# Loads of the first phase held back, the activation table loaded at once, statistics moved between down projections, a second diagonal buffer

## The reference

```python
h = h + 0.5 * swiglu(rmsnorm(h, g_ffn1), w_ffn1_gate, w_ffn1_up, w_ffn1_down)
u = rmsnorm(h, g_mix)
c_q, ckv_pe, q_s, k_s, v_s = split(u @ w_in)            # 1024 -> 1184
o_mla = mla_group(c_q, ckv_pe, ...)    # 8 heads, causal, low-rank q and kv, rotary part
o_swa = swa_group(q_s, k_s, v_s, sinks, rel_bias)        # 8 heads, window 128, sinks, bias
h = h + concat(rmsnorm(o_mla), rmsnorm(o_swa)) @ w_o
h = h + 0.5 * swiglu(rmsnorm(h, g_ffn2), w_ffn2_gate, w_ffn2_up, w_ffn2_down)
return rmsnorm(h, g_final)
```

## Time and profile before

| | us |
|---|---|
| median of 3 runs | 5028.68 (5026.57 to 5029.12) |
| the profiled execution, its own time | 5025.74 |
| its span on the slowest core | 5024.2 (cores: 5007.0 to 5024.2) |
| TensorE matmuls busy | 4873.9 |
| VectorE / ScalarE busy | 2806.6 / 1896.1 |
| DMA packets, mean rate | 751.86 MB, 150 GB/s |

### The profile page before, as it was taken

How to read it: one execution, slowest core, us unless ns; L and a number is a source line. 1 busy time by engine, 2 the same in 40 slices (tenths; PEclk the granted TensorE clock), 3 DMA queues, 4 the chain that set the end, 5 groups by cost and what they waited for, 6 DMA issues and landing times.

```text
span 5024.2 us, 93692 instructions; the slowest of 8 cores (5007.0 to 5024.2 us)
## 1 busy us (share of the span) xinstructions
PE 4873.9 (97%) x29784; PEld 2355.2 (47%) x29784; DVE 2806.6 (56%) x6312; ACT 1896.1 (38%) x3566; POOL 91.4 (2%) x154
## 2 busy tenths in 40 slices
PE   6899999999999999999999999999999999999988
PEld 2344444445444444544544444454544444445443
DVE  4356574554665565564557555565455655655554
ACT  1114435436333342534524243352642323335541
POOL 1100000000000000000000000000000000000000
PEclk9999999999999999999999999999999999999999
DMA  8884754544445454444445445454444545443424
GB/s 177 166 213 128 195 151 145 168 136 148 139 141 178 142 162 148 150 141 130 155 141 176 141 133 176 135 156 148 132 149 144 172 147 170 139 138 116 132 85 141
DMA packets 259289, 751.86 MB, mean 150 GB/s; under 512 B 28320, under 2 KB 36640, under 8 KB 258464
## 3 DMA queue, kind: packets, MB, share of 16 engines
q1 hardware_dynamic: 229664, 648.78, 41.6%
q0 software_dynamic: 28864, 97.07, 8.5%
q10 hardware_dynamic: 288, 0.03, 0.0%
HBM read 716.99 MB, written 73.92 MB: 157 GB/s over the span
## 4 chain that ended last, share of the span: by engine, by line
PE 94%; DMA 3%; DVE 2%; issue 1%; ACT 0%; SPq 0%; DVEq 0%; ACTq 0%; POOL 0%; POOLq 0%
PE ps L558 47%; PE ps L590 23%; PE ps L725 5%; PE ps L879 5%; PE ps L1032 4%; PE ps L899 3%; DVE sb_u L526 1%; PE ps L932 1%; PE ps L817 1%; DMA sb_h<-xT 1%; PE ps L563 1%; PE ps L429 1%; PE ps L442 1%; PE ps L958 1%; DMA sb_slotM<-wms 1%
## 5 line engine op out<-in xcount | busy, mean ns | idle before, releaser
L558 PE MATMUL ps<-sb_u,sb_slotA 128*128 128x512 bf16 x10688 | 2617.1, 381 | 27.3 <-DVE sb_tb L577 18.9
L558 PEld LDWEIGHTS ps<-sb_u,sb_slotA 128*128 128x128 bf16 x10688 | 1001.7, 98 | 1099.0 <-issue 58.3
L590 PE MATMUL ps<-sb_act,sb_slotB 128*128 128x512 bf16 x5632 | 1329.5, 380 | 7.5 <-DMA sb_slotB<-wd 7.4
L577 DVE SCALAR_TENSOR_TENSOR sb_tb<-sb_tb,ps 128x512 f32<-128x512 f32 x704 | 483.0, 686 | 724.9 <-PE ps L558 364.0
L573 ACT ACTIVATE sb_tb<-ps 128x512 f32<-128x512 f32 x704 | 419.7, 596 | 1174.5 <-PE ps L558 954.6
L884 ACT ACTIVATE sb_PT<-ps 128x512 bf16<-128x512 f32 (+3 forms) x1280 | 653.4, 532 | 506.7 <-PE ps L879 401.5
L590 PEld LDWEIGHTS ps<-sb_act,sb_slotB 128*128 128x128 bf16 x5632 | 536.9, 98 | 607.3 <-issue 14.9
L580 DVE TENSOR_TENSOR sb_act<-sb_tb,ps 128x512 bf16<-128x512 f32 x704 | 483.3, 687 | 246.6 <-PE ps L558 204.2
L597 DVE SCALAR_TENSOR_TENSOR sb_h<-ps,sb_h 128x512 f32<-128x512 f32 x544 | 375.7, 691 | 407.5 <-PE ps L590 358.6
L879 PE MATMUL ps<-sb_QT,sb_KT 128*128 128x512 bf16 (+3 forms) x1280 | 426.0, 347 | 0.0
L899 PEld LDWEIGHTS ps<-sb_VA,sb_PT 128*128 128x128 bf16 x4352 | 254.6, 98 | 196.5 <-issue 0.8
(11 more groups left out here) (116 smaller groups left out, 2930.1 us busy)
## 6 DMA issues: line engine op xcount, KB each, us to landing
sb_slotA<-wgu2s SPq DMA_DIRECT2D x340, 512.0 KB, 3.5
sb_slotA<-wgu1s SPq DMA_DIRECT2D x308, 512.0 KB, 3.8
sb_slotM<-wms SPq DMA_DIRECT2D x318, 256.0 KB, 2.9
sb_slotB<-wd2s SPq DMA_DIRECT2D x120, 384.0 KB, 3.2
sb_slotB<-wd1s SPq DMA_DIRECT2D x112, 384.0 KB, 3.2
sb_slotB<-wd2s SPq DMA_DIRECT2D x124, 320.0 KB, 2.9
sb_slotB<-wd1s SPq DMA_DIRECT2D x112, 320.0 KB, 3.0
outT<-sb_h POOLq DMA_DIRECT2D x30, 1024.0 KB, 7.8
```

What stands on the lines that cost most here:

```text
L558: inst = nc.tensor.matmul(PS[bank][:], lhsT=w[:, a, kc, :], rhs=ub[:, kc, :], start=(kc == 0), stop=(kc == 7))
L577: G.op("dve", [("tb", t), P(gb)], [("tb", t)], lambda: nc.vector.scalar_tensor_tensor(out=tb[:, t, :], in0=tb[:, t, :], scalar=1.0, in1=PS ...
L590: inst = nc.tensor.matmul(PS[bank][:], lhsT=w[:, c, :], rhs=act1[:, a0 + c, :], start=(c == 0), stop=(c == nch - 1))
```

## The change

Seven edits, all in one program text.

1. The mixer's first 13 weight items (`m_item`), which had no condition, now wait until chunk 13 + i // 2 of tile 0. Five of them stood at the head of the POOL queue. The table `rope` of the first mixer waits for chunk 16, `mi` and `bt` (the bias of the window group) for chunk 12. The x load of tile 2 waits for chunk 9 in place of 10 and has an earlier `vt`.
2. In the planner an x load of a tile from 2 on counts as landed 15 us later (`slack`), so what uses it is placed later in the engines' lists.
3. A one-element Exp on ScalarE stands ahead of the first x square; the activation table is loaded with it.
4. Two VectorE memsets cover only the columns that need the value 1.
5. `sb_dgF` has two buffers. `sb_dgM` still has one.
6. In the blocks (0, 2), (1, 0), (1, 13) and (1, 14) the Tanh and VectorE operations have `vt = fpos - 10` in place of `fpos - 1000`.
7. The last `final_out` has `vt = fpos - 25` in place of `fpos + 1`.

```diff
+LEAD_E = 10.0
...
-    def dma(self, eng, sem, reads, writes, out, in_, nbytes, vt=None):
+    def dma(self, eng, sem, reads, writes, out, in_, nbytes, vt=None, slack=0.0):
...
-        o.slack = 0.0
+        o.slack = slack
...
-                    r = done
+                    r = done + o.slack
...
-        dgF = sb("dgF", [128, 4, 128], BF16)
-        dgM = sb("dgM", [128, 4, 128], BF16)
+        dgF = sb("dgF", [128, 2, 4, 128], BF16)
+        dgM = sb("dgM", [128, 1, 4, 128], BF16)
...
-                      w * 128 * T * 4, vt=vt + i * 0.01)
+                      w * 128 * T * 4, vt=vt + i * 0.01, slack=15.0 if n >= 2 else 0.0)
...
+        G.op("dve", [], [("ssq", 0)], lambda: nc.vector.memset(ssq[:, 0, 0:1], 0.0), 0.1, vt=-6000)
+        G.op("act", [("ssq", 0)], [("ssq", 0)], lambda: nc.scalar.activation(
+            out=ssq[:, 0, 0:1], in_=ssq[:, 0, 0:1], func=AF.Exp), 1.5, vt=-6000)
         G.dma("act", "snk", [], [("esink",)], esink[:], sinks_in.partition_broadcast(128), 4096, vt=-4000)
         G.op("act", [("esink",)], [("esink",)],
              lambda: nc.scalar.activation(out=esink[:], in_=esink[:], func=AF.Exp), 0.2, vt=100)
         G.op("dve", [], [("ksz", b, g, x) for b in range(5) for g in range(2) for x in range(2)],
              lambda: nc.vector.memset(ksz[:], 0.0), 0.6, vt=50)
-        G.op("dve", [], [("VS", b) for b in range(5)], lambda: nc.vector.memset(VS[:], 1.0), 0.4, vt=50)
-        G.op("dve", [], VAALL, lambda: nc.vector.memset(VA[:], 1.0), 4.0, vt=60)
+        G.op("dve", [], [("VS", b) for b in range(5)], lambda: nc.vector.memset(VS[:, :, :, 64:65], 1.0), 0.2, vt=50)
+        G.op("dve", [], VAALL, lambda: nc.vector.memset(VA[:, :, :, 64:65], 1.0), 0.4, vt=60)
...
+            nd = dg.shape[1]
             for part in range(2):
-                G.op("dve", [(tag + "b",), ("ident",)], [dkey], lambda part=part: nc.vector.tensor_tensor(
-                    out=dg[:], in0=ident[:].unsqueeze(1).to_broadcast([128, 4, 128]),
+                x = part % nd
+                G.op("dve", [(tag + "b",), ("ident",)], [dkey + (x,)], lambda part=part, x=x: nc.vector.tensor_tensor(
+                    out=dg[:, x, :, :], in0=ident[:].unsqueeze(1).to_broadcast([128, 4, 128]),
                     in1=nwb[:, part, 0:4].unsqueeze(2).to_broadcast([128, 4, 128]), op=ALU.mult), 0.7)
-                G.op("pe", [dkey, ("ones",)], [P(bank)], lambda part=part: nc.tensor.matmul(
-                    PS[bank][:], lhsT=onesb[:], rhs=dg[:].rearrange("p j t -> p (j t)"),
+                G.op("pe", [dkey + (x,), ("ones",)], [P(bank)], lambda part=part, x=x: nc.tensor.matmul(
+                    PS[bank][:], lhsT=onesb[:], rhs=dg[:, x, :, :].rearrange("p j t -> p (j t)"),
...
+        lead = [1000.0]
...
-                    dv = fpos[0] - 1000
+                    dv = fpos[0] - lead[0]
...
-                    op1=ALU.add), d_dve(512), vt=fpos[0] - 1000)
+                    op1=ALU.add), d_dve(512), vt=fpos[0] - lead[0])
...
-                G.dma("pool", f"Mc{s}", [], keys, view, wm_in[i], 575000)
+                G.dma("pool", f"Mc{s}", [("pace", 0, 0, 13 + i // 2)], keys, view, wm_in[i], 575000)
...
-            G.dma("sp", "rope", [], [R[0], R[1]], rope[:].rearrange("p a t -> p (a t)"), rope_in[ti], 524288)
+            G.dma("sp", "rope", [("pace", 0, 0, 16)] if n == 0 else [], [R[0], R[1]], rope[:].rearrange("p a t -> p (a t)"), rope_in[ti], 524288)
...
-        load_x(2, 2, "sp", 130, [("pace", 0, 0, 10)])
-
-
-        G.dma("sp", "bt", [("pace", 0, 0, 6)], [("Bb", hd) for hd in range(8)], Bb[:].rearrange("p w h q -> p (w h q)"), bt_in,
+        load_x(2, 2, "sp", 80, [("pace", 0, 0, 9)])
+
+
+        G.dma("sp", "bt", [("pace", 0, 0, 12)], [("Bb", hd) for hd in range(8)], Bb[:].rearrange("p w h q -> p (w h q)"), bt_in,
               1048576, vt=90)
-        G.dma("sp", "mi", [("pace", 0, 0, 5)], [("W", 0)], mi[:].rearrange("p w q -> p (w q)"), cst_in[:, 256:512], 131072, vt=89)
+        G.dma("sp", "mi", [("pace", 0, 0, 12)], [("W", 0)], mi[:].rearrange("p w q -> p (w q)"), cst_in[:, 256:512], 131072, vt=89)
...
+            lead[0] = LEAD_E if (f, n) in ((0, 2), (1, 0), (1, NT - 3), (1, NT - 2)) else 1000.0
...
-        final_out(NT - 1, fpos[0] + 1, True)
+        final_out(NT - 1, fpos[0] - 25, True)
```

## The result

The changed kernel takes 4986.1 us (median) against 5028.7. The ratio of the means is 0.9913, with an interval of 0.9893 to 0.9932: 43.8 us less, between 34 and 54. Forecast were 4991 us and a gain of 38. Executions in which the cores of a die ran at a lower clock are left out everywhere in what follows, and a mean over the cores takes in only undisturbed dies.

The account below looks back on a forecast made before the run. TensorE's matmuls were busy 4873.9 of 5024.2 us, leaving at most 150 us. First phase 24, last mixer 12 and tail 2 sum to 38 us off 5025.7: 4987.7, plus 3 for the median, 4991; range 4981 to 4999.

Parts of the forecast that it names:

- Start and tile 1: At the kernel's start, earlier x landings and first gates of tiles 0 and 1 win 15 us, between 9.5 and 20.
- Tile 2: At tile 2's first squares, the 16.95 us stall on its x load shrinks to perhaps 2; 13 us won, 0 to 18.5.
- What the held-back loads cost later: Up to 300 us, nearly full DMA engines make weights late in places; 4 us taken off, leaving 24.
- the start is given back: Casts at 180 to 300 us make down weights and slot writes late; 15 us return, 23 won, 5006; chance 0.12.
- Second diagonal buffer: Saves a 0.84 us wait at start, last mixer and tail; nothing in the middle, where matmuls hide it.
- Last mixer: At the last mixer's end, matmuls cover waits of 2.93, 2.01 and 4.71 us; 12 us won, 6 to 17.
- Tail: After the last addition to h, sums end 2.0 us sooner and the diagonal gives 0.84; net 2 us won.
- Table load: The 1.28 us load ahead of the first x square moves earlier; its gain is counted within the start's 8.7 us.
- rival of another table: The early Exp loads a table without Tanh, each switch costs 1.28 us, total above 5300 us; chance 0.01.
- Priority in (0, 2), (1, 0): In these blocks and (1, 13), order moves with nothing that can be priced: 0 us, between -4 and +4.
- Slower: In four blocks, 88 Tanhs each wait for one more ScalarE operation; 53 us lost, 5044; chance 0.03.
- no net change: Tile 2's x still late, the start's gain returned and half the last mixer's gain lost, together; chance 0.06.

Follow-up runs that it names:

- e7_slack0: Changed kernel without the later belief in x landings, so an x load counts as landed as early as before; ratio 0.9951 to the kernel before.
- e6_precast: Changed kernel with the first phase's eight DRAM-to-DRAM casts moved into block (0, 2); 4985.08 us, a single time.
- e8_split: Changed kernel with four of the eight DRAM-to-DRAM casts at chunks 17 to 20, four behind the mixer's last weights in (0, 2); ratio 0.9872 to the kernel before.
- e2_start: Kernel before with only the mixer's casts, rope, mi and bt held back, the Exp at the head and the small memsets; ratio 0.9988.
- e3_x2: Kernel before with only tile 2's x load released by chunk 9 and x loads from tile 2 on counted as landed 15 us later; ratio 1.0006.
- e1_diag: Kernel before with two buffers for sb_dgF and nothing else changed; ratio 0.9967.
- e5_nodiag: Changed kernel with one sb_dgF buffer again, all other edits kept; ratio 0.9952 to the kernel before.
- e11_leadlate: Changed kernel with the lower Tanh and VectorE priority in blocks (1, 13) and (1, 14) only; ratio 0.9922 to the kernel before.
- r_after: The changed kernel, unaltered, run again on another chip as comparison for the experiments; ratio 0.9907 to the kernel before.

## Why the prediction came out as it did

The time, 4986.1 against 4991, and the gain, 43.8 against 38, agree. The terms do not. On the five cores of the table the sum reads 17.8 (24 forecast) for the first phase, 16.5 (0) for the middle, 10.3 (12) for the last mixer and 2.5 (2) for the tail. The 6 us that the start fell short were more than made up by 16 that were forecast nowhere. That the total came near is luck.

- *Start and tile 1, 15*: 20 at Tanh 16, the upper end. The last square of tile 0 begins at 13.65, as the third of the group that starts at 12.39 (near 12.5 forecast), the first gate at 21.83 (21), tile 1's at 46.83 (42 to 46). The limit that I drew from 15.4 us of lighter DMA work did not bind at this place yet.
- *Tile 2, 13*: 31.5 less 20, so 11.5. There is a stall of 5.39 us at the second half, and 2.4 behind it. The load was as slow as forecast (30 and 39 us), and the place in the list won what was won, as e7_slack0 shows: without edit 2 the stall is 19.1 us. What the prediction had wrong here is that it took the 35 us to landing as given. On core 4 e6_precast and e8_split have 9 to 13 and 22 to 24 us, and no wait for x.
- *What the held-back loads cost later, 4*: 14 (31.5 to 17.8). This is the term that was too small, and its name is not right either. The rival "the start is given back" had its size, with casts falling at 180 to 300 us. But e2_start and e3_x2 show that each lead is lost by itself (12 and 11 us), and e3_x2 holds no cast back at all, so the loss is not the price of holding loads back. With the eight casts from DRAM to DRAM gone from the phase (by the price of the earlier trace rows an estimated 31 us of work), or four gone and four at 223 us and later, the lead at Tanh 44 is 23 us greater. I had let the lead fill nearly all of the 29 us that full DMA engines would have allowed; but they still stood idle 29 us of the first 300 (32 before), so little of that room was used. A bound from the sum of the work does not say when a single load lands. The three parts of the start together: 17.8 in place of 24.
- *Second diagonal buffer, "in the middle matmuls of the block hide it, nothing there"*: this step failed, and with it the mechanism of the middle. The buffer was worth 16 us in all, by two experiments (e1_diag, e5_nodiag), of which the table has most between 450 and 4440 us. I read that TensorE did not wait at the diagonals and took the chain for hidden. I should have followed it one step on, to the next thing that TensorE waited for, `sb_u`, whose waits came to 18.1 us in the trace of the kernel before and fell to 8.7.
- *Last mixer, 12*: 10.3, with 2.88 us of the wait left.
- *Tail, 2*: 2.5; the last sum begins 0.98 us behind the last addition's end (1.1).
- *Table load*: at 1.57 us, nothing behind 3 us; ahead of all work, as forecast, and its Exp begins 0.01 us behind it. No second load. The rival of another table is out.
- *Priority in (0, 2), (1, 0), 0 (within 4)*: alone nothing. In the whole, some 8 us between Tanhs 66 and 132 hang on it (e11_leadlate), though the total shows 2 by the means and 8 by the ratios. Edit 2 for all tiles makes mixer weights late there (e3_x2), and edit 6 with the second buffer seems to undo it (e5_nodiag, e11_leadlate). How exactly the three lists meet stays open.
- *Slower, no net change*: out.

Of the signs that I had named, "no stall above 6 us at tile 2's squares" and "in the last mixer's end less than 5 us idle" held. "DMA share above 0.95 all through 0 to 270" did not: it reads 0.58 at 160 to 180 us, where SP stood 35 us for the landing of a down weight and issued nothing. Of the signs of being wrong one came: ScalarE stands on `xT` again, for 13.88 and 6.66 us, though most of it cost TensorE nothing. Weights end waits of up to 3.5 us on the profiled core between 150 and 420 us, and of 6.3 us on core 4.

## What to carry to other kernels

A wait that other matmuls cover is not free if it uses up the cover of the next one: follow a chain to the next instruction at which the engine does stand, and count how much independent work is left behind it. Where the DMA engines are nearly full, a lead won at the front of the phase was lost at its end. What kept it was to take casts that nothing waits for out of the stretch in which loads are waited for, and not to put them beside the next phase's first loads. A planner that believes in an early landing puts a waiting instruction ahead of work that could run; to correct its belief was worth 12 us with a load that stayed slow. Look also at what is issued beside such a load: without three casts there, tile 2's halves landed 14 to 26 us sooner.

## What the runs showed of the hardware

- Tile 2's x halves (1 MB each, issued together) landed 30 and 39 us later in the profiled execution, 2.1 MB for which the engines need an estimated 6.6 us of work at the price of SP's queue. Three casts from DRAM to DRAM issued within 19 us ahead of it and beside it go with that: with them the halves take 30 to 36 and 38 to 41 us on the eight cores (r_after), without them 8 to 15 and 17 to 27 us (e6_precast). By the price of the earlier trace rows the three casts are an estimated 12 us of work, less than the 14 to 26 us by which the halves came sooner.
- A 512 KB load on SP went from 7.2 to 29.1 us to landing when four casts from DRAM to DRAM were issued within 12 us beside it (e6_precast). I had counted such casts by their share of the DMA engines alone, and not by what they do to the latency of a load.
- Holding the five casts and `rope` back brought tile 0's last chunk 7.6 us sooner: its square began at 21.26 after a wait for the landing, and begins at 13.65 without one. On the five cores of the table the landing is 7.7 to 9.9 us earlier. The Trainium skill, page "DMA: Bandwidth & Descriptors", section "Queues, rings and completion order", says that an engine takes turns between the queue rows that have work; the prediction's estimate by that was 6.6 us, and the traces have more.
